# Cross attention of a two-block transformer kernel: heads made as channels, exponentials scaled before their transposes, and a weights unit moved between logits and transposes

## The chip, the cores and the metric

One core of a Trainium2 chip. The metric is the device time of one execution in microseconds (us), median of the runs. Everything is float32: matrix products of streamed weights are made in three passes of split numbers (high x high, high x low, low x high, marked fp32r), attention products in plain float32.

## What is computed

The kernel computes two transformer layers' worth of blocks on 256 tokens of width 1024. The part that the change touches is the memory cross attention of the first block:

```python
def memory_cross_attention(x, mem, norm_g, mem_g, wq, wk, wv, wo):
    h = rms_norm(x, norm_g)
    m = rms_norm(mem, mem_g)
    q = (h @ wq).reshape(B_, S, MEM_HEADS, MEM_HEAD_DIM)     # 4 heads of 256
    k = (m @ wk).reshape(B_, M, MEM_HEADS, MEM_HEAD_DIM)     # 256 memory rows
    v = (m @ wv).reshape(B_, M, MEM_HEADS, MEM_HEAD_DIM)
    logits = jnp.einsum('bshd,bmhd->bhsm', q, k) * (MEM_HEAD_DIM ** -0.5)
    p = jax.nn.softmax(logits, axis=-1)
    o = jnp.einsum('bhsm,bmhd->bshd', p, v)
    return o.reshape(B_, S, MEM_HEADS * MEM_HEAD_DIM) @ wo
```

The second block has memory attentions of its own, whose keys and values come from `a_mem_kv_2` and `b_mem_kv_2`; the kernel makes them early, beside this cross attention.

## The kernel before

**The stream of weights.** All weights pass through a ring of 4 places in units of 128 x 2048 numbers (1 MB). SP issues the transfer of unit u once unit u-4 is used. ACT copies it to the high part (`hi`, L2321, `w_hi`), DVE subtracts to get the low part (`lo`, L1497, `w_lo`), PE multiplies. On ACT and DVE the helper `product(name, i)` of unit u asks for the parts up to unit u+2 (AHEAD = 3). Each engine executes its own instructions strictly in the order in which the program lists them; the order of the work is therefore the order of the calls in `tensor_program`, `vector_program`, `scalar_program`, and semaphores (`Signal`) join them.

**The stage of the cross attention.** Queries (`cross_qT`) and keys (`cross_kT`) lie as channels (partitions) by tokens, values (`cross_v`) as rows. Around the attention the jobs `kv_m0` and `kv_m1` (two units each) make keys and values of the second block's memories in banks 0 and 1; `one_unit` (L898, L1734, L2470) hands out one unit per call, and before `kv_m1` begins PE waits until `kv_m0` has been copied out of the banks (`kept`): its keys by ACT (`memory_keys`, L2574), then its values by DVE (`memory_values`, L1846). The first unit of `kv_m0` runs on PE ahead of the attention; the other three are called from `attention("c", ...)` (L995, L1853, L2582).

In `attention` (L849, L1650, L2428) a head i goes through these steps, the steps of heads i, i-1 and i-2 lying in one pass i of the loop:
- PE makes the logits, 128 queries x 256 memory rows for each of two token tiles, in bank 4 or 5 (L859).
- DVE takes the maximum of each row (L1705), scaled by the inverse rms (L1711); ACT takes exponentials with their sums (L2441).
- PE transposes the exponentials in four blocks of 128 x 128 (L880, waits for the exponentials); ACT copies them to `weights_t` (L2459).
- PE multiplies, transposed exponentials stationary and values moving, giving tokens x 256 columns of the head (L893).
- DVE has made the inverse of the sums (L1661) and scales the head by it on the way out of the bank to `xn` (L1726, signal `o`).

The pass ends with `unit()`. In PE's pass 0 there is no unit, since the first has gone ahead; on ACT and DVE pass 0 has one, behind exponentials 0 and maxima 0.

**Behind the attention.** PE transposes the 16 blocks of `xn` (`turns("oc", ...)`, L998, executed at L697), ACT and DVE split them out of the banks to `oc_channels_hi` and `oc_channels_lo` (L2356, L1533), PE transposes the keys of the two memories (`heads_turned("mk0"/"mk1")`, 8 blocks, L843), and the output projection `co0`, `co1` (L1006, L1007) follows with the channels of `oc` moving.

Of the kernel before, what the change touches and what calls it, by code (L numbers as in the profile page):

```python
# [7 lines left out]
F32 = mybir.dt.float32  # L8
# [186 lines left out]
TURNS = {"mix": FULL, "mem": FULL, "mixed": FULL, "mem2": FULL, "oc": FULL, "lat": [(0, 0, 2), (1, 0, 2)],  # L195
# [5 lines left out]
class Kernel:  # L201
# [7 lines left out]
    def signals(self):  # L209
# [94 lines left out]
        self.o = Signal(nc, "heads_out", **iters)  # L304
        self.weighed = Signal(nc, "exps_normed", l=MLA_HEADS)
# [57 lines left out]
    def memory(self):  # L363
# [13 lines left out]
        def in_channels(name, kb, shape):  # L377
# [46 lines left out]
                   for n, kb in (("mixed", 64), ("oc", 8), ("bmix", 33))}  # L424
# [254 lines left out]
def tensor_program(k):  # L679
    nc, PE, bank, ident = k.nc, k.nc.tensor, k.bank, k.ident[:, :]  # L680

    def matmul(out, lhs, rhs, start, stop):
        return nc.tensor.matmul(out, lhs, rhs, start=start, stop=stop)  # L683
# [165 lines left out]
    def attention(tag, between=None, after=0):  # L849
        n, step, spans, off, total, dv = k.attention(tag)  # L850
        bias = ATTENTIONS[tag][2]
        for i in range(n + 2 + after):
            if i < n and tag in ("c", "l"):
                if i >= 2:
                    PE.wait_ge(*(k.maxed if bias else k.exped).at(tag, i - 2))
                for tok in range(NT):
                    for kk in range(2 if tag == "c" else 1):
                        lhs, rhs = k.logit_operands(tag, i, tok, kk)
                        m = matmul(bank[4 + i % 2][:, off[tok]:off[tok] + spans[tok]], lhs, rhs, kk == 0, tag != "c" or kk == 1)  # L859
                m.then_inc(k.qk.sem, 1)  # L860
            elif i < n and (step == 2 or i % 2 == 0):

                h0 = i * step
                for h in (h0, h0 + 1):
                    if h >= 2:
                        PE.wait_ge(*(k.maxed if bias else k.exped).at(tag, h - 2))
                for tok in range(NT):
                    for h in (h0, h0 + 1):
                        lhs, rhs = k.logit_operands(tag, h, tok, 0)
                        m = matmul(bank[4 + h % 2][:, off[tok]:off[tok] + spans[tok]], lhs, rhs, True, True)  # L870
                        if tok == NT - 1:
                            m.then_inc(k.qk.sem, 1)
# [122 lines left out]
    attention("c", lambda i: unit() if i else None)  # L995
    PE.wait_ge(*k.exped.all("c"))
    PE.wait_ge(*k.pt.all("c"))
    turns("oc", (0, 1, 2, 3), k.o.all("c"))  # L998
    kept("kv_m0")
    kept("kv_m1")  # L1000
    for n in range(2):
        PE.wait_ge(*k.ch_hi.at("oc", n))
        PE.wait_ge(*k.ch_lo.at("oc", n))
        heads_turned(f"mk{n}", [(k.mk_rows[n][:, tok, b * P:(b + 1) * P], P) for b in range(2) for tok in range(NT)], (4 + n,))
    PE.wait_ge(*k.o.all("c"))
    channel_job("co0", k.OC["oc"], "oc")  # L1006
# [486 lines left out]
def vector_program(k):  # L1493
# [156 lines left out]
    def attention(tag, between=None, finish=None):  # L1650
# [3 lines left out]
        def stat(j):  # L1654
            return k.stats[:, j % 4, :]
# [26 lines left out]
        def maxima(heads):  # L1682
            for h in heads:
# [25 lines left out]
                if tag == "c":  # L1709
                    V.wait_ge(*k.rstd_done.all("cross"))  # L1710
                    r = V.tensor_tensor(stat(h)[:, 0:2], stat(h)[:, 0:2], k.rstd_cols("cross"), ALU.mult)  # L1711
                else:
                    r = V.tensor_scalar(stat(h)[:, 0:2], stat(h)[:, 0:2], scale, None, ALU.mult)
                r.then_inc(k.maxed.sem, 1)
# [138 lines left out]
    attention("c", lambda i: unit())  # L1853
    channels_lo("oc", (0, 1, 2, 3))
# [462 lines left out]
def scalar_program(k):  # L2317
# [110 lines left out]
    def attention(tag, between=None, finish=None):  # L2428
        n, step, spans, off, total, dv = k.attention(tag)
        bias = ATTENTIONS[tag][2]  # L2430
        def exponentials(heads):
            for h in heads:
# [7 lines left out]
                for tok in range(NT):  # L2440
                    e = A.activation(E[:, off[tok]:off[tok] + spans[tok]], L[:, off[tok]:off[tok] + spans[tok]], ACT.Exp,  # L2441
                                     bias=stat[:, tok:tok + 1],
                                     scale=-1.0 if bias else k.rstd_cols("cross")[:, tok:tok + 1] if tag == "c" else k.scale_of(tag),
# [138 lines left out]
    attention("c", lambda i: unit())  # L2582
    channels_hi("oc", (0, 1, 2, 3))
    for n in range(2):
        heads_copied(f"mk{n}", 0, k.mem_kT[n][:, :, :])
    residual_job("co0", 0)
# [541 lines left out]
```

## Time and profile before

| | |
|---|---|
| median of 3 runs | 1156.02 us (1154.36 to 1156.06) |
| the profiled execution's own time | 1156.42 us |
| its span, first to last instruction | 1155.1 us |
| PE busy | 1117.1 us (97%), clock 0.992 of full |
| PE weight load busy | 1063.4 us (92%) |
| DVE, ACT, POOL busy | 732.8, 569.0, 73.4 us |
| 16 DMA engines | 182.70 MB, mean 158 GB/s |

The time of the profiled execution is its span and 1.3 us around it. PE is busy nearly throughout; the ends of its matmuls are modelled by the profiler, so pace is better read from start to start. A matmul of float32 operands shows as two instructions in the trace.

### The profile page before, as it was taken

What the parts mean: (1) busy time and instruction counts of PE and PEld (TensorE: products, weight loads), DVE (VectorE), ACT (ScalarE), POOL (GpSimd) and SP (SyncE); (2) the same over time, 40 slices, a digit from 0 to 9 for tenths busy, and PEclk for the clock granted to TensorE, in tenths of its full rate; (3) what the DMA queues carried; (4) which work ended last, traced back from release to release, by engine and by line L of the source; (5) the groups of instructions that cost most, each with busy time, mean ns of one, the idle gap of its engine ahead of it and who ended that gap; (6) DMA issues with size and microseconds to landing.
All of it is one profiled execution on the core that took longest, in us unless ns stands there. A gap on an engine that the chain in (4) does not pass through costs nothing.

```text
span 1155.1 us, 22499 instructions
## 1 busy us (share of the span) xinstructions
PE 1117.1 (97%) x9837; PEld 1063.4 (92%) x9837; DVE 732.8 (63%) x1042; ACT 569.0 (49%) x767; POOL 73.4 (6%) x134
## 2 busy tenths in 40 slices
PE   8999999999999999999799999999999999999998
PEld 8888889789999999988688999999987889999998
DVE  5557657455665556767988756555577875655553
ACT  6355646344544444684344634434365774443343
POOL 2410111100000000400000000000002000000000
PEclk9999999999999999998999999999999999999999
DMA  7933444325455554533000445555554224555551
GB/s 263 311 145 125 162 166 172 142 90 186 183 190 189 186 183 182 198 125 136 12 3 3 162 180 184 187 184 192 188 198 151 105 76 181 185 185 186 188 189 55
DMA packets 29862, 182.70 MB, mean 158 GB/s; under 512 B 3591, under 2 KB 6872, under 8 KB 8900
## 3 DMA queue, kind: packets, MB, share of 16 engines
q1 hardware_dynamic: 24608, 174.07, 41.8%
q0 software_dynamic: 1888, 4.75, 1.5%
q10 hardware_dynamic: 3268, 2.43, 0.7%
q8 instruction: 78, 1.28, 0.5%
q14 instruction: 20, 0.16, 0.0%
HBM read 180.18 MB, written 1.07 MB: 157 GB/s over the span
## 4 chain that ended last, share of the span: by engine, by line
PE 82%; DVE 7%; ACT 5%; issue 3%; POOL 2%; DMA 1%; ACTq 0%; DVEq 0%; POOLq 0%
PE bank L683 79%; ACT w_hi L2329 2%; DVE w_lo L1503 1%; DMA w_raw<-in_weights 1%; PE bank L697 1%; PE bank L880 1%; ACT exps L2441 1%; DVE inverse L2219 1%; DVE inverse_t L2244 0%; POOL inverse_rms_diagonals L2872 0%; DMA bias_rows<-bias_lines 0%; PE bank L687 0%; DVE chunk_products L2199 0%; PE bank L1225 0%; ACTq L2516 0%
## 5 line engine op out<-in xcount | busy, mean ns | idle before, releaser
L1503 DVE TENSOR_TENSOR w_lo<-w_raw,w_hi 128x2048 fp32r<-128x2048 f32 x157 | 358.0, 2291 | 200.1 <-ACT w_hi L2329 199.8
L2329 ACT ACTIVATE w_hi<-w_raw 128x2048 fp32r<-128x2048 f32 x161 | 306.5, 1913 | 111.4 <-DMA w_raw<-in_weights 106.2
L683 PE MATMUL bank<-x_channels_hi,w_hi 128*128 128x256 f32 x1424 | 230.8, 286 | 3.8 <-DVE proj L1575 1.3
L683 PE MATMUL bank<-x_channels_lo,w_hi 128*128 128x256 f32 x1424 | 228.3, 284 | 0.0
L683 PE MATMUL bank<-x_channels_hi,w_lo 128*128 128x256 f32 x1424 | 220.8, 278 | 0.0
L683 PEld LDWEIGHTS bank<-x_channels_hi,w_hi 128*128 128x128 f32 x1424 | 196.2, 192 | 7.6 <-issue 3.9
L683 PEld LDWEIGHTS bank<-x_channels_lo,w_hi 128*128 128x128 f32 x1424 | 194.2, 191 | 0.1
L683 PEld LDWEIGHTS bank<-x_channels_hi,w_lo 128*128 128x128 f32 x1424 | 191.7, 189 | 0.0
L683 PE MATMUL bank<-hidden_hi,w_lo 128*128 128x256 f32 x528 | 103.6, 284 | 0.0
L683 PE MATMUL bank<-hidden_hi,w_hi 128*128 128x256 f32 x528 | 102.0, 281 | 0.0
L683 PE MATMUL bank<-hidden_lo,w_hi 128*128 128x256 f32 x528 | 101.7, 280 | 0.0
L683 PEld LDWEIGHTS bank<-hidden_lo,w_hi 128*128 128x128 f32 x528 | 79.7, 188 | 0.0
L683 PEld LDWEIGHTS bank<-hidden_hi,w_hi 128*128 128x128 f32 x528 | 79.2, 188 | 0.5 <-issue 0.5
L683 PEld LDWEIGHTS bank<-hidden_hi,w_lo 128*128 128x128 f32 x528 | 79.5, 188 | 0.0
L2598 ACT ACTIVATE gates<-gates 128x512 f32<-128x512 f32 x33 | 20.9, 632 | 91.1 <-DVE gates L1877 91.1
L2602 ACT ACTIVATE hidden_hi<-values 128x512 fp32r<-128x512 f32 x33 | 20.9, 632 | 90.6 <-DVE values L1884 90.6
L1879 DVE TENSOR_TENSOR values<-bank,inverse_rms_rows 128x512 f32<-128x512 f32 x33 | 22.7, 689 | 40.7 <-PE bank L683 40.7
L1877 DVE TENSOR_TENSOR gates<-bank,inverse_rms_rows 128x512 f32<-128x512 f32 x33 | 22.6, 684 | 24.9 <-ACT inverse_rms_rows L2422 24.9
L1886 DVE TENSOR_TENSOR hidden_lo<-values,hidden_hi 128x512 fp32r<-128x512 f32 x33 | 22.9, 693 | 23.1 <-ACT hidden_hi L2602 23.1
L2885 POOL TENSOR_SCALAR channel_inverse_rms<-channel_mean_squares 128x2 f32<-128x2 f32 x5 | 1.2, 231 | 552.3 <-DVE channel_mean_squares L1644 552.3
L2403 ACT ACTIVATE x_channels_hi<-x,gain_columns 128x256 fp32r<-128x256 f32 x40 | 17.7, 500 | 33.3 <-DVE x L1606 33.3
L1606 DVE TENSOR_TENSOR x<-bank,x 128x512 f32<-128x512 f32 x28 | 19.0, 687 | 21.9 <-PE bank L683 21.8
(450 smaller groups left out, 1550.1 us busy)
## 6 DMA issues: line engine op xcount, KB each, us to landing
w_raw<-in_weights SPq DMA_DIRECT2D x163, 1024.0 KB, 4.8
mem_rows<-in_mem POOLq DMA_DIRECT2D x2, 1024.0 KB, 6.1
xn<-in_x SPq DMA_DIRECT2D x1, 1024.0 KB, 5.5
w_raw<-in_weights SPq DMA_DIRECT2D x2, 512.0 KB, 8.6
bias<-bias_rows ACTq DMA_DIRECT2D x2, 512.0 KB, 9.1
bias<-bias_rows ACTq DMA_DIRECT2D x1, 1024.0 KB, 11.0
out<-xn SPq DMA_DIRECT2D x4, 256.0 KB, 2.5
wide_masks<-in_triangle_masks POOLq DMA_DIRECT2D x1, 832.0 KB, 8.3
```

What stands on the lines that cost most here:

```text
L683: return nc.tensor.matmul(out, lhs, rhs, start=start, stop=stop)
L697: t = nc.tensor.transpose(b[:, j * P:(j + 1) * P], k.turn_source(stage, tok, k0 + j), ident)
L880: m = nc.tensor.transpose(b[:, c:c + P], e[:, c:c + P], ident)
L1503: V.tensor_tensor(k.w_lo[:, s, :], k.w_raw[:, s, :], k.w_hi[:, s, :].bitcast(F32), ALU.subtract).then_inc(k.lo_done, 1)
L1606: V.tensor_tensor(k.x[:, b:b + 2, :], k.product_bank(name, n).rearrange("p (k t) -> p k t", k=2), k.x[:, b:b + 2, :], ALU.add).then_inc(k. ...
L1877: V.tensor_tensor(k.gates[:, par, :, :], pairs(2 * par), R, ALU.mult).then_inc(k.gate_scaled.sem, 1)
L1879: V.tensor_tensor(k.values[:, par, :, :], pairs(2 * par + 1), R, ALU.mult).then_inc(k.up_scaled.sem, 1)
L1886: V.tensor_tensor(k.HL[:, par, :, :], k.values[:, par, :, :], k.HH[:, par, :, :].bitcast(F32), ALU.subtract).then_inc(k.hid_lo.sem, 1)
L2329: A.activation(k.w_hi[:, s, :], k.w_raw[:, s, :], ACT.Copy).then_inc(k.hi_done, 1)
L2403: A.activation(high[:, b, :], k.x[:, b, :], ACT.Copy, scale=k.split_gain(stage, part, b)).then_inc(k.x_hi.sem, 1)
L2598: A.activation(k.gates[:, par, :, :], k.gates[:, par, :, :], ACT.Silu).then_inc(k.silu.sem, 1)
L2602: A.activation(k.HH[:, par, :, :], k.values[:, par, :, :], ACT.Copy).then_inc(k.hid_hi.sem, 1)
```

## The change

Cross attention no longer uses the general `attention`; each engine gets its own order, head by head. The head's output is made as channels x tokens at once: values stationary (two blocks of 128 channels), transposed exponentials moving (256 tokens, picked from `weights_t` in two runs of 128), so the 16 transposes of `xn` and the scaled copy to `xn` go. The exponentials are scaled by their inverse sums in SBUF before they are transposed. ACT and DVE split each head from its bank (`cross_heads_hi`, `cross_heads_lo`). On PE the second unit of `kv_m0` stands between the logits of head 1 and the transposes of head 0. On ACT and DVE the first `unit()` stands ahead of exponentials and maxima 0, and both of heads 0 and 1 ahead of the second. The `oc` channels move to other places of SBUF.

```diff
@@ -192 +192 @@
-TURNS = {"mix": FULL, "mem": FULL, "mixed": FULL, "mem2": FULL, "oc": FULL, "lat": [(0, 0, 2), (1, 0, 2)],
+TURNS = {"mix": FULL, "mem": FULL, "mixed": FULL, "mem2": FULL, "lat": [(0, 0, 2), (1, 0, 2)],
          "qlat": [(0, 0, 4), (1, 0, 4)], "bmix": [(0, 6, 2), (1, 6, 2)]}
 SPLITS = {"cross": 1, "ffn0": 1, "n1": 1, "ffn1": 1, "kvb": 2, "ffn2": 1}
@@ -301,8 +301,10 @@
...
-        self.o = Signal(nc, "heads_out", **iters)
-        self.weighed = Signal(nc, "exps_normed", l=MLA_HEADS)
+        self.o = Signal(nc, "heads_out", **{**iters, "c": 0})
+        self.weighed = Signal(nc, "exps_normed", c=4, l=MLA_HEADS)
+        self.cross_hi = Signal(nc, "cross_heads_hi", c=4)
+        self.cross_lo = Signal(nc, "cross_heads_lo", c=4)
...
@@ -421,7 +423,8 @@
...
+        self.OC["oc"] = (work("oc_channels_hi", 40, [P, KT, S], F32R), work("oc_channels_lo", 72, [P, KT, S], F32R))
...
@@ -850,15 +853,7 @@
         n, step, spans, off, total, dv = k.attention(tag)
...
-            if i < n and tag in ("c", "l"):
-                if i >= 2:
-                    PE.wait_ge(*(k.maxed if bias else k.exped).at(tag, i - 2))
-                for tok in range(NT):
-                    for kk in range(2 if tag == "c" else 1):
-                        lhs, rhs = k.logit_operands(tag, i, tok, kk)
-                        m = matmul(bank[4 + i % 2][:, off[tok]:off[tok] + spans[tok]], lhs, rhs, kk == 0, tag != "c" or kk == 1)
-                m.then_inc(k.qk.sem, 1)
-            elif i < n and (step == 2 or i % 2 == 0):
+            if i < n and (step == 2 or i % 2 == 0):
...
@@ -992,18 +987,57 @@
...
-    attention("c", lambda i: unit() if i else None)
-    PE.wait_ge(*k.exped.all("c"))
-    PE.wait_ge(*k.pt.all("c"))
-    turns("oc", (0, 1, 2, 3), k.o.all("c"))
+    def cross_logits(h):
+        if h >= 2:
+            PE.wait_ge(*k.exped.at("c", h - 2))
+        for tok in range(NT):
+            for kk in range(2):
+                lhs, rhs = k.logit_operands("c", h, tok, kk)
+                m = matmul(bank[4 + h % 2][:, tok * S:(tok + 1) * S], lhs, rhs, kk == 0, kk == 1)
+        m.then_inc(k.qk.sem, 1)
+    def cross_exps_turned(h):
+        PE.wait_ge(*k.weighed.at("c", h))
+        if h >= 2:
+            PE.wait_ge(*k.pt.at("c", h - 2))
+        e = k.exps("c", h)
+        for c in range(0, NT * S, P):
+            m = nc.tensor.transpose(bank[6 + h % 2][:, c:c + P], e[:, c:c + P], ident)
+        m.then_inc(k.e_turned.sem, 1)
+    def cross_values(h):
+        PE.wait_ge(*k.pt.at("c", h))
+        if h >= 2:
+            PE.wait_ge(*k.cross_lo.at("c", h - 2))
+        pt = k.ptbuf[:, (h % 2) * 512:(h % 2) * 512 + NT * S].rearrange("p (t j c) -> p t j c", t=NT, j=2)
+        for b in range(2):
+            for j in range(2):
+                m = matmul(bank[2 + h % 2][:, b * S:(b + 1) * S].rearrange("p (t c) -> p t c", t=NT),
+                           k.cross_v[:, j, 256 * h + P * b:256 * h + P * (b + 1)], pt[:, :, j, :], j == 0, j == 1)
+        m.then_inc(k.pv.sem, 1)
+    cross_logits(0)
+    for i in range(1, 4):
+        cross_logits(i)
+        unit()
+        cross_exps_turned(i - 1)
+        if i >= 2:
+            cross_values(i - 2)
+    cross_exps_turned(3)
+    cross_values(2)
     kept("kv_m0")
     kept("kv_m1")
+    PE.wait_ge(*k.exped.all("c"))
     for n in range(2):
-        PE.wait_ge(*k.ch_hi.at("oc", n))
-        PE.wait_ge(*k.ch_lo.at("oc", n))
         heads_turned(f"mk{n}", [(k.mk_rows[n][:, tok, b * P:(b + 1) * P], P) for b in range(2) for tok in range(NT)], (4 + n,))
-    PE.wait_ge(*k.o.all("c"))
-    channel_job("co0", k.OC["oc"], "oc")
+    cross_values(3)
+    PE.wait_ge(*k.cross_lo.at("c", 1))
+    channel_product("co0", 0, k.OC["oc"])
+    PE.wait_ge(*k.cross_lo.at("c", 3))
+    channel_product("co0", 1, k.OC["oc"])
     channel_job("co1", k.OC["oc"])
...
@@ -1850,8 +1879,52 @@
...
-    attention("c", lambda i: unit())
-    channels_lo("oc", (0, 1, 2, 3))
+    def cross_maxima(h):
+        stat = k.stats[:, h, :]
+        V.wait_ge(*k.qk.at("c", h))
+        for tok in range(NT):
+            k.dve.mark(V.tensor_reduce(out=stat[:, tok:tok + 1], in_=bank[4 + h % 2][:, tok * S:(tok + 1) * S], axis=AX.X, op=ALU.max,
+                                       negate=True))
+        V.wait_ge(*k.dve.so_far())
+        V.wait_ge(*k.rstd_done.all("cross"))
+        V.tensor_tensor(stat[:, 0:2], stat[:, 0:2], k.rstd_cols("cross"), ALU.mult).then_inc(k.maxed.sem, 1)
+    def cross_exps_normed(h):
+        stat, E = k.stats[:, h, :], k.exps("c", h)
+        V.wait_ge(*k.exped.at("c", h))
+        V.reciprocal(stat[:, 4:6], stat[:, 2:4]).then_inc(k.inverse.sem, 1)
+        V.wait_ge(*k.inverse.at("c", h))
+        for tok in range(NT):
+            cols = slice(tok * S, (tok + 1) * S)
+            r = V.tensor_scalar(E[:, cols], E[:, cols], stat[:, 4 + tok:5 + tok], None, ALU.mult)
+            if tok == 0:
+                k.dve.mark(r)
+        r.then_inc(k.weighed.sem, 1)
+    def cross_heads_lo(h):
+        high, low = k.OC["oc"]
+        V.wait_ge(*k.cross_hi.at("c", h))
+        V.tensor_tensor(low[:, 2 * h:2 * h + 2, :], bank[2 + h % 2][:, :].rearrange("p (k t) -> p k t", k=2),
+                        high[:, 2 * h:2 * h + 2, :].bitcast(F32), ALU.subtract).then_inc(k.cross_lo.sem, 1)
+    unit()
+    cross_maxima(0)
+    cross_maxima(1)
+    cross_exps_normed(0)
+    cross_exps_normed(1)
+    unit()
+    cross_maxima(2)
+    cross_exps_normed(2)
+    unit()
+    cross_maxima(3)
+    cross_heads_lo(0)
+    cross_exps_normed(3)
+    unit()
+    for h in range(1, 4):
+        cross_heads_lo(h)
...
@@ -2579,10 +2652,52 @@
...
-    attention("c", lambda i: unit())
-    channels_hi("oc", (0, 1, 2, 3))
+    def cross_exps(h):
+        E, stat = k.exps("c", h), k.stats[:, h, :]
+        A.wait_ge(*k.maxed.at("c", h))
+        if h >= 2:
+            A.wait_ge(*k.e_turned.at("c", h - 2))
+        for tok in range(NT):
+            cols = slice(tok * S, (tok + 1) * S)
+            e = A.activation(E[:, cols], bank[4 + h % 2][:, cols], ACT.Exp, bias=stat[:, tok:tok + 1],
+                             scale=k.rstd_cols("cross")[:, tok:tok + 1], accum_out=stat[:, 2 + tok:3 + tok])
+            if tok == 0:
+                k.act.mark(e)
+        e.then_inc(k.exped.sem, 1)
+    def cross_exps_kept(h):
+        A.wait_ge(*k.e_turned.at("c", h))
+        if h >= 2:
+            A.wait_ge(*k.pv.at("c", h - 2))
+        at = (h % 2) * 512
+        A.activation(k.ptbuf[:, at:at + NT * S], bank[6 + h % 2][:, :], ACT.Copy).then_inc(k.pt.sem, 1)
+    def cross_heads_hi(h):
+        A.wait_ge(*k.pv.at("c", h))
+        A.activation(k.OC["oc"][0][:, 2 * h:2 * h + 2, :], bank[2 + h % 2][:, :].rearrange("p (k t) -> p k t", k=2),
+                     ACT.Copy).then_inc(k.cross_hi.sem, 1)
+    unit()
+    cross_exps(0)
+    cross_exps(1)
+    unit()
+    cross_exps_kept(0)
+    cross_exps(2)
+    unit()
+    cross_exps_kept(1)
+    cross_exps(3)
+    cross_heads_hi(0)
+    unit()
+    cross_exps_kept(2)
+    cross_heads_hi(1)
+    cross_exps_kept(3)
+    cross_heads_hi(2)
     for n in range(2):
         heads_copied(f"mk{n}", 0, k.mem_kT[n][:, :, :])
+    cross_heads_hi(3)
     residual_job("co0", 0)
     residual_job("co1", 4)
```

## Rows read from the trace of the kernel before

**Rows 1.** The page: chain that ended last by engine; DMA issues, us to landing.

```profile
PE 82%; DVE 7%; ACT 5%; issue 3%; POOL 2%; DMA 1%; ACTq 0%; DVEq 0%; POOLq 0%
...
w_raw<-in_weights SPq DMA_DIRECT2D x163, 1024.0 KB, 4.8
```

**Rows 2.** Busy time of each engine in the stage: us, PE, PEld, DVE, ACT, POOL, PEclk, DMA.

```profile
212.20:251.20 39.00, 35.89 (x178) 29.50 (x176) 19.12 (x32) 18.13 (x33) 0.00 (x0) 1.00 0.30 108
```

**Rows 3.** Timeline of PE: start us, us, engine line op operands, [idle before <-releaser].

```profile
212.20 3.62 PE L683 MATMUL bank<-cross_kT,cross_qT 128*128 128x256 f32 x16
216.37 0.66 PE L880 MATMUL bank<-ident,exps 128*128 128x128 f32 x4 [0.55 <-ACT exps L2441]
216.78 1.18 PE L683 MATMUL bank<-w_hi,mem_channels_hi 128*128 128x512 f32 x4
...
222.44 1.89 PE L683 MATMUL bank<-cross_kT,cross_qT 128*128 128x256 f32 x8
224.16 0.60 PE L880 MATMUL bank<-ident,exps 128*128 128x128 f32 x4
224.60 1.89 PE L683 MATMUL bank<-cross_v,weights_t 128*128 128x256 f32 x8
227.98 1.20 PE L683 MATMUL bank<-w_hi,mem_channels_hi 128*128 128x512 f32 x4 [1.49 <-DVE mem_v L1850]
...
243.56 3.62 PE L683 MATMUL bank<-cross_v,weights_t 128*128 128x256 f32 x16
248.05 1.94 PE L697 MATMUL bank<-ident,xn 128*128 128x128 f32 x16 [0.88 <-DVE xn L1726]
250.18 1.23 PE L843 MATMUL bank<-ident,mem_k_rows 128*128 128x128 f32 x8 [0.19 <-DVE oc_channels_lo L1533]
251.16 0.72 PE L683 MATMUL bank<-oc_channels_hi,w_hi 128*128 128x256 f32 x4
```

**Rows 4.** Timeline of ACT in the same stage.

```profile
215.11 0.56 ACT L2441 ACTIVATE exps<-bank,stats,channel_inverse_rms 128x256 f32<-128x256 f32 x1 [10.52 <-DVE stats L1711]
...
216.21 1.91 ACT L2329 ACTIVATE w_hi<-w_raw 128x2048 fp32r<-128x2048 f32 x1
...
221.33 0.56 ACT L2441 ACTIVATE exps<-bank,stats,channel_inverse_rms 128x256 f32<-128x256 f32 x1 [3.22 <-DVE stats L1711]
...
224.71 0.84 ACT L2579 ACTIVATE mem_k_rows<-bank,row_inverse_rms 128x256 f32<-128x256 f32 x2
```

**Rows 5.** Timeline of DVE in the same stage.

```profile
214.12 0.75 DVE L1705 TENSOR_REDUCE stats<-bank 128x1 f32<-128x256 f32 x2 [6.62 <-PE bank L683]
...
218.14 2.29 DVE L1503 TENSOR_TENSOR w_lo<-w_raw,w_hi 128x2048 fp32r<-128x2048 f32 x1 [3.07 <-ACT w_hi L2329]
220.35 0.74 DVE L1705 TENSOR_REDUCE stats<-bank 128x1 f32<-128x256 f32 x2
...
224.85 2.29 DVE L1503 TENSOR_TENSOR w_lo<-w_raw,w_hi 128x2048 fp32r<-128x2048 f32 x1 [3.48 <-ACT w_hi L2329]
227.06 0.87 DVE L1850 TENSOR_SCALAR mem_v<-bank,row_inverse_rms 128x256 f32<-128x256 f32 x2
```

**Rows 6.** Groups of DVE between 800 and 1000 us: xcount | busy us, mean ns.

```profile
L2025 DVE TENSOR_SCALAR exps<-exps,stats 128x256 f32<-128x256 f32 x12 | 4.2, 347 | 0.0
```

**Rows 7.** Groups between 205 and 256 us: `oc` split by DVE and ACT, reciprocals.

```profile
L1533 DVE TENSOR_TENSOR oc_channels_lo<-bank,oc_channels_hi 128x512 fp32r<-128x512 f32 x4 | 2.5, 682 | 1.4 <-ACT oc_channels_hi L2356 1.4
...
L2356 ACT ACTIVATE oc_channels_hi<-bank 128x512 fp32r<-128x512 f32 x4 | 2.1, 602 | 4.4 <-PE bank L697 4.4
...
L1661 DVE RECIPROCAL stats<-stats 128x2 f32<-128x2 f32 x4 | 0.6, 157 | 0.0
```

**Rows 8.** Timeline of PE at an earlier block of transposes.

```profile
154.37 1.06 PE L697 MATMUL bank<-ident,xn 128*128 128x128 f32 x8 [0.89 <-ACT cross_v L2381]
156.66 1.68 PE L697 MATMUL bank<-ident,xn 128*128 128x128 f32 x8 [1.23 <-DVE xn L1826]
```

**Rows 9.** Busy time of each engine around those transposes, columns as in rows 2.

```profile
155.00:160.00 5.00, 3.77 (x21) 3.54 (x20) 3.29 (x6) 3.30 (x5) 1.82 (x4) 0.70 0.92 327
```

More of the change, by code:

```diff
@@ L423, in memory @@
         self.OC = {n: (work(f"{n}_channels_hi", kb, [P, KT, S], F32R), work(f"{n}_channels_lo", kb + 8, [P, KT, S], F32R))
-                   for n, kb in (("mixed", 64), ("oc", 8), ("bmix", 33))}
+                   for n, kb in (("mixed", 64), ("bmix", 33))}
+        self.OC["oc"] = (work("oc_channels_hi", 40, [P, KT, S], F32R), work("oc_channels_lo", 72, [P, KT, S], F32R))
         self.OC["amix"] = (work("amix_channels_hi", 36, [P, KT, S], F32R), work("amix_channels_lo", 60, [P, KT, S], F32R))
@@ L1708, in maxima @@
                 V.wait_ge(*k.dve.so_far())
[L1709 to L1714, printed above, removed]
+                V.tensor_scalar(stat(h)[:, 0:2], stat(h)[:, 0:2], scale, None, ALU.mult).then_inc(k.maxed.sem, 1)
         for i in range(n + 2 + (finish is not None)):
@@ L2442, in exponentials @@
                                      bias=stat[:, tok:tok + 1],
-                                     scale=-1.0 if bias else k.rstd_cols("cross")[:, tok:tok + 1] if tag == "c" else k.scale_of(tag),
+                                     scale=-1.0 if bias else k.scale_of(tag),
                                      accum_out=stat[:, 2 + tok:3 + tok])
```

## The prediction

> **What bounds the kernel now.** I read the page first: PE makes 82% of the chain that ended last [rows 1], so a saving counts only where it shortens PE's own row of work. The busy shares by stage come next: in the cross attention's 39.0 us, from its first logits to the first product of `co0`, PE shows 35.9 us busy at full clock (1.00), DVE 19.1 and ACT 18.1 [rows 2]. The waits are thus few, but there are some, and PE's timeline puts four of them in their places [rows 3]: 0.55 us for the exponentials of head 0, 1.49 us for `mem_v`, 0.88 us for the last scaled head in `xn`, 0.19 us for the `oc` split. The timelines of ACT and DVE say where the largest is from. Maxima 0 end before 215.1, exponentials 0 run to 216.2, and only behind them does ACT make a `w_hi` (216.21) [rows 4] and DVE its `w_lo` (218.14); maxima 1, though their logits have been ready since 216, stand behind that until 220.35, and so exponentials 1 until 221.33, the next `w_hi`, the next `w_lo` until 224.85, and `mem_v` until 227.06 [rows 4, 5]. PE must not start `kv_m1` ahead of `mem_v`, and starts at 227.98.
>
> **PE's work after the change, by pace.** Starts give these prices [rows 3]: a head's logits 1.72 us (222.44 to 224.16, 8 instructions at 0.215), four transposes 0.44 us (224.16 to 224.60), a unit of `kv_m` about 5.6 us (216.78 to 222.44, less a few hundredths at its start). A head's values are 8 instructions of the same shape and the same shown length as the logits (1.89 us for 8 in both rows), so 1.72. The eight transposes of memory keys cost 0.87 at 0.108 each; their 0.98 (250.18 to 251.16) has a small wait in it.
> What stays is 4 x 1.72 of logits, 4 x 1.72 of values, 4 x 0.44 of transposes, 3 units x 5.6, and 0.87: 33.2 us. With no wait anywhere `co0` starts at 212.20 + 33.2 = 245.4. It starts at 251.16 now. The difference is **5.75 us**. From the other side: the 16 transposes of `xn` are 1.7 us, the four waits 3.1 us, and about 0.9 us are the drains that come with a wait (the next instruction starts some 0.2 us after the pace of those before it would let it) and the slower first instructions behind one. So both ways agree.
>
> **Is there really no wait?** This is the step on which all hangs, so I carried the three queues forward together, with a hand-over from PE of 0.2 us (logits 0 are paced out at 213.92, the maxima start at 214.12 [rows 3, 5]) and of 0.03 between ACT and DVE.
> - *The first unit moved ahead.* Its `w_hi` and `w_lo` are for two units on. The transfer is issued when the unit four before is used, that is two units of 5.6 us ahead of 212.2, near 201, and lands 4.8 us later [rows 1], at 206. ACT sat idle for 10.52 us before 215.11 and DVE for 6.62 before 214.12 [rows 4, 5], so the 1.9 and 2.3 us fit there for nothing. Were they late, logits 0 would wait with them; there are 4 us to spare.
> - *Heads 0 and 1.* Maxima 0 at 214.12, exponentials 0 to 216.2; maxima 1 at 215.84 in place of 220.35, exponentials 1 at 216.83 to 217.9. The scalings of exponentials are new: two instructions of 0.35 us each [rows 6] behind a reciprocal of 0.16 us [rows 7], 0.9 us a head. Head 0 is scaled by 217.7, head 1 by 218.9. PE, meanwhile at logits 1 and then the second unit of `kv_m0` until 221.24, wants head 0 at 221.24: 3.5 us of cover. The 0.55 us wait is gone with the unit that now lies there.
> - *The narrow place.* ACT's next `w_hi` runs 217.9 to 219.85, then the keys of `kv_m0`, the second at 221.41 (unit's end and hand-over) to 221.9; DVE's `w_lo` 219.9 to 222.15, then two `mem_v`, 0.87 us [rows 5], to 223.0. PE has turned head 0 (221.68) and made logits 2 (223.40) by then: 0.4 us to spare, where 1.49 us were waited.
> - *Head 3*, whose scaling on DVE is behind the low part of head 0: logits 3 end at 232.9, maxima to 234.05, exponentials to 235.15, ACT's high part of head 0 0.60 us, DVE's low part 0.68 us [rows 7], scaling to 237.4. PE wants it at 240.6.
> - *The end.* `kept` of the second unit of `kv_m1` at 240.9, wanted at 242.8; `weights_t` of head 2 at 239.7, wanted at 241.1; of head 3 at 242.05, wanted at 243.7. `co0`'s first half needs heads 0 and 1 (split at 242.2), its second half head 3, split at 246.9 and wanted 5.6 us after the first, at 251.0. That split moved to the cover of `co0`; ACT's and DVE's parts for `co1`, which stand behind it, come as long after the start of `co0` as now, some 7 us, and are wanted at 11.
> ACT trades four copies (`oc`) for four of the same size, DVE four scaled copies to `xn` and four splits for eight scalings and four splits: the scalings cost 3.5 us a stage, the `xn` copies were 2.7, on an engine that has 20 us free in this stage [rows 2]. No transfer is added or moved; SP's queue follows PE.
> **Behind the stage** nothing is tied to absolute time: every transfer is issued on PE's progress. I take the whole 5.75 us to the end, since PE makes the chain there too.
>
> **A rule weighed against the rows.** From 247.0 (the pace of the last values) to 251.16 PE of before does only transposes and waits, and the granted clock is 1.00 throughout [rows 2, 3]. Around 154 to 158 it did the same, 16 transposes with idle time between, and there the clock went to its lower level (1.2 of 2.4 GHz; 0.70 as mean of 5 us, so 5 x 0.30 = 1.5 us lost) [rows 8, 9]. The change takes the 4 us stretch away.
> The Trainium skill's page "TensorE: Matmul & The Clock Gate", section "Part 4: PE-mode transpose", says that transposes don't count as PE being busy for the clock. By that rule executions of before can lose clock at 247 to 251 too, and the saving would be about 7.3 us; the trace of this stage disagrees (1.00), that of 154 to 158 agrees.
>
> **New and unseen in the trace: the moving operand in two runs of 128.** The values product now streams `weights_t` in two pieces of 512 B, 1 KB apart, and writes a bank through a two-part pattern. No row shows a float32 product so fed. Bounds: nothing (the same 8 instructions of 256 columns), or twice the pace, 6.9 us in all for 32 instructions [rows 3]; less than nothing is excluded, for the columns streamed are the same. I take nothing: the nearest row is the values product itself.
>
> **The sum.** 1156.42 (the profiled execution) - 5.75 = 1150.67. That execution stood 0.4 us above the median of the runs, so the median goes from 1156.02 to **1150.3**.
>
> **Rivals.**
> 1. *A wait comes back in part.* The narrow place is 0.4 us wide. If exponentials 1 or the `w_hi` behind them come 2 us later than I have it, PE waits 1.6 us for `mem_v` again, as it waited 1.49; a like slip can happen at `weights_t` of head 2 (1.4 us to spare). 1156.02 - 4.1 = 1151.9. For: in-order queues with many hand-overs. Against: each duration is measured in this very stage.
> 2. *More than forecast.* Where before's ordinary runs lose clock in the transposes at 247 to 251, 1.5 us more are saved: 1148.8. For: the lowest run is 1.7 us under the median, about one such loss. Against: the profiled execution has no loss there and is not faster than the others.
> 3. *Slower.* The values products, in their new form, run at half pace, as between the two bounds above. They lie on PE's own row with nothing to cover them: +6.9 - 5.75 = +1.15 us, 1157.2. It decides from about 0.18 us more per instruction (5.75 / 32) on a pace of 0.215. Against: nothing in the rows; the pace of products here is set by the columns.
> 4. *The change does not do what it says:* the transposes of the exponentials now wait for DVE, not for ACT, and the saved waits return as waits for DVE. For: four such waits are new. Against: cover of 3 us at each. It would leave only the `xn` transposes and their waits, some 3.2 us (from 247.0 to 250.18): 1152.8.
>
> **How the numbers follow.** Forecast 0.70, rival 1 0.11, rival 2 0.09, rival 3 0.03, rival 4 0.07. A measurement of this kernel can tell about 0.2% from no change, 2.3 us. All but rival 3 are faster by more than that, if rivals 1 and 4 do not go together with other slips; I give the same 0.06, slower 0.02. The range takes in rival 1 and rival 2 and about half of rival 4: 1148.6 to 1152.5.
>
> **What would show it.** In the changed profile: no `PE L697` group on `xn` in this stage; `co0`'s first product 33 us behind the first logits; PE's waits between them under 0.5 us; values products at 0.215 us each from start to start; scalings at 0.35 us and maxima 1 directly behind maxima 0; `mem_v` of `kv_m0` done within 0.4 us of the end of logits 2. A values row of 8 instructions that takes 3.4 us to the next start would prove rival 3, a wait for `mem_v` or `weights_t` rival 1, a wait for the scaled `exps` rival 4. A span behind `co0` that differs from before's by over 1 us would say that the saving is not carried to the end.

## The result, and the profile after

| | before | after |
|---|---|---|
| median of 4 runs each, side by side | 1155.71 us (1154.36 to 1156.06) | 1148.26 us (1147.11 to 1149.09) |
| ratio, 95% interval | | 0.9937 (0.9920 to 0.9954) |
| the profiled execution's own time | 1156.42 us | 1147.55 us |
| its span | 1155.1 us | 1146.2 us |
| first logits to first product of `co0` | 38.96 us | 32.99 us |

Faster by 0.63%, or 7.5 us between these medians. The prediction was 1150.3 us, with a range from 1148.6: the direction and nearly all of the mechanism came out as forecast, and the time lies 0.3 us below the range.

The page after, chain by engine and the transfers of weights, answers to [rows 1]: PE still sets the end, and no transfer was touched.

```profile
PE 83%; DVE 7%; ACT 4%; issue 2%; POOL 2%; DMA 1%; ACTq 0%; DVEq 0%; POOLq 0%
...
w_raw<-in_weights SPq DMA_DIRECT2D x163, 1024.0 KB, 4.8
```

Busy time in the stage after, from the first logits to `co0`, with the columns of [rows 2]:

```profile
211.06:244.05 32.99, 32.99 (x162) 27.91 (x160) 17.14 (x34) 16.78 (x32) 0.00 (x0) 1.00 0.35 128
```

PE shows as busy in all 32.99 us. Its timeline after shows the new order, and no row in it carries an idle time in brackets, where [rows 3] had four:

```profile
211.06 3.62 PE L686 MATMUL bank<-cross_kT,cross_qT 128*128 128x256 f32 x16
214.32 1.28 PE L686 MATMUL bank<-w_hi,mem_channels_hi 128*128 128x512 f32 x4
...
220.09 0.60 PE L1007 MATMUL bank<-ident,exps 128*128 128x128 f32 x4
220.53 1.89 PE L686 MATMUL bank<-cross_kT,cross_qT 128*128 128x256 f32 x8
222.07 1.27 PE L686 MATMUL bank<-w_hi,mem_channels_hi 128*128 128x512 f32 x4
...
227.82 0.60 PE L1007 MATMUL bank<-ident,exps 128*128 128x128 f32 x4
228.26 1.89 PE L686 MATMUL bank<-weights_t,cross_v 128*128 128x256 f32 x8
229.99 1.89 PE L686 MATMUL bank<-cross_kT,cross_qT 128*128 128x256 f32 x8
231.53 1.29 PE L686 MATMUL bank<-w_hi,mem_channels_hi 128*128 128x512 f32 x4
...
237.30 0.60 PE L1007 MATMUL bank<-ident,exps 128*128 128x128 f32 x4
237.74 1.89 PE L686 MATMUL bank<-weights_t,cross_v 128*128 128x256 f32 x8
239.47 0.60 PE L1007 MATMUL bank<-ident,exps 128*128 128x128 f32 x4
239.90 1.89 PE L686 MATMUL bank<-weights_t,cross_v 128*128 128x256 f32 x8
241.63 1.04 PE L846 MATMUL bank<-ident,mem_k_rows 128*128 128x128 f32 x8
242.50 1.89 PE L686 MATMUL bank<-weights_t,cross_v 128*128 128x256 f32 x8
244.05 0.81 PE L686 MATMUL bank<-oc_channels_hi,w_hi 128*128 128x256 f32 x4
```

ACT's timeline after (against [rows 4]): the first `w_hi` has gone into the idle time ahead of the attention, and exponentials 1 stand directly behind exponentials 0.

```profile
204.41 1.92 ACT L2402 ACTIVATE w_hi<-w_raw 128x2048 fp32r<-128x2048 f32 x1 [0.96 <-DMA w_raw<-in_weights]
213.97 0.56 ACT L2663 ACTIVATE exps<-bank,stats,channel_inverse_rms 128x256 f32<-128x256 f32 x1 [7.64 <-DVE stats L1891]
...
215.70 0.56 ACT L2663 ACTIVATE exps<-bank,stats,channel_inverse_rms 128x256 f32<-128x256 f32 x1 [0.52 <-DVE stats L1891]
...
216.79 1.92 ACT L2402 ACTIVATE w_hi<-w_raw 128x2048 fp32r<-128x2048 f32 x1
```

DVE's timeline after (against [rows 5]): maxima 1 at 214.71 behind maxima 0 at 212.98, the scalings, then `w_lo` and `mem_v`, which end at 221.83. PE starts `kv_m1` at 222.07. That 0.24 us is the narrow place that the prediction named.

```profile
206.36 2.29 DVE L1537 TENSOR_TENSOR w_lo<-w_raw,w_hi 128x2048 fp32r<-128x2048 f32 x1
212.98 0.76 DVE L1887 TENSOR_REDUCE stats<-bank 128x1 f32<-128x256 f32 x2 [4.33 <-PE bank L686]
...
214.71 0.76 DVE L1887 TENSOR_REDUCE stats<-bank 128x1 f32<-128x256 f32 x2 [0.78 <-PE bank L686]
...
215.77 0.62 DVE L1901 TENSOR_SCALAR exps<-exps,stats 128x256 f32<-128x256 f32 x2
...
218.75 2.29 DVE L1537 TENSOR_TENSOR w_lo<-w_raw,w_hi 128x2048 fp32r<-128x2048 f32 x1 [1.00 <-ACT w_hi L2402]
220.96 0.87 DVE L1879 TENSOR_SCALAR mem_v<-bank,row_inverse_rms 128x256 f32<-128x256 f32 x2
```

**The rest of the time.** The span fell by 8.9 us, the stage by 5.97. The other 2.9 us lie ahead of the stage (1.1 us) and behind it (1.8 us), where PE's order is unchanged. Much of this follows the granted clock. Three stretches of before, with the columns of [rows 2]:

```profile
150.00:165.00 15.00, 12.88 (x81) 11.65 (x81) 10.64 (x11) 7.77 (x12) 2.66 (x6) 0.89 0.49 180
520.00:535.00 15.00, 15.00 (x85) 13.24 (x84) 11.59 (x17) 9.37 (x11) 0.00 (x0) 0.77 0.32 108
...
870.00:880.00 10.00, 8.14 (x39) 6.81 (x38) 8.03 (x10) 3.98 (x7) 4.06 (x5) 0.83 0.30 107
```

and the same of after:

```profile
150.00:165.00 15.00, 12.88 (x93) 11.56 (x92) 10.98 (x12) 8.10 (x12) 2.99 (x7) 1.00 0.54 192
515.00:530.00 15.00, 15.00 (x100) 13.61 (x100) 13.50 (x23) 9.56 (x16) 0.00 (x0) 0.89 0.32 123
...
870.00:880.00 10.00, 9.20 (x48) 6.91 (x47) 7.11 (x25) 8.06 (x16) 0.96 (x2) 1.00 0.53 193
```

Length times (1 - clock) gives the loss of a stretch: about 1.7, 3.4 and 1.7 us in before's profiled execution, 0, 1.7 and 0 in after's. Is that a gift of the change, or of the one execution that was profiled? The copies below answer most of this.

### The profile page after: what moved, and what is told of

The parts are those of the page before. It is cut to its first block, busy times and chain, and to the rows that moved or that the text cites. A ratio compares the mean times of both kernels' runs of the same rounds, so it can differ in the third digit from the quotient of the medians.

```text
span 1146.2 us, 22461 instructions
## 1 busy us (share of the span) xinstructions
PE 1112.4 (97%) x9821; PEld 1060.4 (93%) x9821; DVE 733.3 (64%) x1046; ACT 569.4 (50%) x767; POOL 73.4 (6%) x134
## 3 DMA queue, kind: packets, MB, share of 16 engines
HBM read 180.18 MB, written 1.07 MB: 158 GB/s over the span
## 4 chain that ended last, share of the span: by engine, by line
PE 83%; DVE 7%; ACT 4%; issue 2%; POOL 2%; DMA 1%; ACTq 0%; DVEq 0%; POOLq 0%
PE bank L686 80%; DVE w_lo L1537 1%; ACT w_hi L2402 1%; DMA w_raw<-in_weights 1%; PE bank L700 1%; PE bank L875 1%; DVE inverse L2292 1%; DVE inverse_t L2317 0%; ACT exps L2514 0%; POOL inverse_rms_diagonals L2987 0%; DMA bias_rows<-bias_lines 0%; PE bank L690 0%; DVE chunk_products L2272 0%; PE bank L1259 0%; PE bank L1278 0%
```

## The experiments

Every kernel ran beside runs of the kernel before on the same chip. "Stage" is always the first logits to the first product of `co0`, by PE's timeline.

### Both kernels again, unchanged: e1_before_again, e8_before_third, e11_before_fourth, e2_after_again, e9_after_third, e10_after_fourth

No edit. These show what one kernel's profile and median do from copy to copy.

> The kernel before once more, unchanged, for its spread and for where its clock falls. In the two first profiles the stage from the first logits to co0 took 38.96 us before and 32.99 after, 5.97 less, but the spans differ by 8.9 and the medians by 7.45. Theory A (chance): the 1.5 to 3 us that are left are granted clock lost at places that differ from execution to execution (before: near 155, 525, 571, 873 us; after: near 525, 568, 1133). Then this profile has another set of such places than the first, and time plus half-clock loss (span x (1 - mean clock)) is near 1147.2 in every execution of this kernel. Theory B (rival 2 of the prediction): ordinary executions of this kernel lose clock at 247 to 255 us, in the transposes that the change takes away. Then this profile shows a clock under 1.00 in that stretch. Theory C: the change costs or gives time outside its stage by itself; then the places are the same as in the first profile, stage by stage.

> The changed kernel once more, unchanged. Stage from first logits to co0 again 33.0 us by every theory. A: the places of lost clock differ from those of its first profile, and the ratio over ten or so runs of each moves towards the stage's 5.97 us (0.9948), time less clock loss near 1141.1. B: ratio stays near 0.9937 (7.3 us less), and the places other than 247 to 255 are as frequent in both kernels. C: same places as in its first profile, none near 155 and 873 us, ratio stays near 0.9937.

> The kernel before a third time, for the number of its executions that lose clock. Theory A: spans differ from those of the changed kernel, at equal loss, by the stage's 5.97 us; this profile again shows no lower clock at 247 to 255 us, and its places of loss differ from the two others. Rival 2: it does show it.

> The changed kernel again, for the 1 us between the stage (5.97 us less in every profile) and the medians (7.45, 6.6 less). Theory A (chance): clock is lost in pieces at the same few loss-prone places in both kernels, which of them are hit differs from execution to execution; over more runs the difference comes down towards 6.0 us, about 0.9948, and segment by segment the profile equals the others but for a piece lost here and there. Theory C (something of the change outside the stage): it stays at 7.

> As the run before it; a second sample on the same chip. By theory A the two samples of the same kernel differ from each other by as much as either from 6.0 us less than before, some tenths to 1 us; by theory C both are 7 us less, alike.

> The kernel before again beside them. By theory A a copy of before differs from before by tenths as well, and its stage is 38.96 to 39.00 us with the clock at 1.00 in it.

| kernel | median (range, runs) | ratio to before, side by side | stage | clock low at (us from start) |
|---|---|---|---|---|
| before | 1155.71 (1154.36-1156.06, 4) | 1 | 38.96 | 157, 526-532, 570, 874, 1154 |
| e1, before | 1155.47 (1152.30-1159.59, 12) | 1.0008 (0.9995-1.0021) | 38.99 | 555, 565-572, 1145 on |
| e8, before | 1154.19 (1152.06-1156.17, 11) | 1.0006 (0.9997-1.0015) | 39.00 | 527, 568, 1145 on |
| e11, before | 1154.30 (1151.98-1157.01, 12) | 0.9997 (0.9987-1.0007) | 38.97 | 553, 567, 1144, 1151 |
| after | 1148.26 (1147.11-1149.09, 4) | 0.9937 (0.9920-0.9954) | 32.99 | 520, 561, 1138 on |
| e2, after | 1147.91 (1146.69-1148.35, 5) | 0.9938 (0.9926-0.9951) | 33.00 | 157, 550, 560-567, 1140 on |
| e9, after | 1147.89 (1146.19-1149.72, 6) | 0.9940 (0.9927-0.9954) | 32.99 | 101, 159, 552, 562-569, 1142 on |
| e10, after | 1146.92 (1146.28-1147.66, 5) | 0.9932 (0.9920-0.9944) | 32.98 | 157, 549, 563, 1140 |

Each place named is a piece of 3.4 us (6.8 where two numbers stand; "on": to the end, less in the last place of before and of e11, which the end cuts off), in which the clock is at its lower level (1.2 of 2.4 GHz). Two stretches of e1, which is the kernel before, and of e2, which is the changed one:

```profile
150.00:165.00 15.00, 12.89 (x93) 11.57 (x92) 10.91 (x12) 8.19 (x12) 3.02 (x8) 1.00 0.55 198
...
870.00:880.00 10.00, 8.62 (x46) 6.93 (x47) 7.41 (x11) 4.92 (x8) 1.97 (x3) 1.00 0.40 144
```

```profile
150.00:165.00 15.00, 12.88 (x82) 11.70 (x81) 10.90 (x11) 7.67 (x12) 2.57 (x6) 0.89 0.46 174
```

At 150 to 165 us the copy of before is at full clock and the copy of after is not: the other way round than in the two profiles above. So the losses there belong to the execution, not to the kernel. The stage, in contrast, is 38.96 to 39.00 in four profiles and 32.98 to 33.00 in four. **The change takes 5.97 us out of the stage.** Of the 2.9 us outside it in the first pair of profiles, much is chance: from `co0`'s first product to the end, the four profiles of before take 901.4 to 904.6 us, those of the changed kernel 901.0 to 902.2. It is not shown that all of it is. The expectations had said that by chance alone the ratio would come towards 0.9948; the places of low clock moved as that theory said, but the ratios stayed at 0.9938, 0.9940 and 0.9932, and the last interval does not hold 0.9948. What is left of this stands under "What stays open".

The clock in the transposes at the end of before's stage is 1.00 in all four profiles. Here e8, from the values of head 2 to well behind `co0`'s start:

```profile
240.00:260.00 20.00, 18.93 (x137) 17.32 (x136) 11.38 (x13) 8.30 (x12) 0.00 (x0) 1.00 0.27 100
```

### e3_rows_back: the form of the heads as before, the new order kept

```diff
-        PE.wait_ge(*k.weighed.at("c", h))
+        PE.wait_ge(*k.exped.at("c", h))
...
-                m = matmul(bank[2 + h % 2][:, b * S:(b + 1) * S].rearrange("p (t c) -> p t c", t=NT),
-                           k.cross_v[:, j, 256 * h + P * b:256 * h + P * (b + 1)], pt[:, :, j, :], j == 0, j == 1)
+                m = matmul(bank[2 + h % 2][:, tok * S:(tok + 1) * S], pt[:, tok * S + j * P:tok * S + (j + 1) * P],
+                           k.cross_v[:, j, 256 * h:256 * h + 256], j == 0, j == 1)
...
     cross_exps_turned(3)
     cross_values(2)
+    cross_values(3)
...
+    turns("oc", (0, 1, 2, 3), k.o.all("c"))
...
-    cross_values(3)
```

with the scaled copies to `xn` and the splits of `oc` as before, and no scaling of exponentials.

> The new order of the three queues kept, but heads made as rows again: exponentials not scaled, transposed exponentials stationary and values moving, head scaled into xn by DVE, 16 transposes of xn, split from there, co0 behind. Theory (PE's row of work sets the time): back come 16 transposes (1.73 us), the wait for the last head in xn (about 0.9), that for the split (0.2), and some 0.3 of drains: stage 33.0 + 3.2 = 36.2 us, 1151.4 us. The waits of 0.55 and 1.49 us stay away. If instead the order alone had given nothing and all came from the form, it would be at the time before, 1155.7. By rival 2 of the prediction another 1.5 us are lost in some executions in the transposes at their new place, 242 to 247 us.

Measured: 1151.13 us (1150.45 to 1152.75, 6 runs), ratio 0.9971 (0.9959 to 0.9984); stage 36.45 us. Its PE timeline has the tail of [rows 3] back, with the same two waits:

```profile
245.29 1.94 PE L700 MATMUL bank<-ident,xn 128*128 128x128 f32 x16 [0.88 <-DVE xn L1904]
247.42 1.23 PE L846 MATMUL bank<-ident,mem_k_rows 128*128 128x128 f32 x8 [0.19 <-DVE oc_channels_lo L1568]
248.40 0.72 PE L686 MATMUL bank<-oc_channels_hi,w_hi 128*128 128x256 f32 x4
```

The form of the heads is worth 36.45 - 32.99 = 3.46 us of the stage: 16 transposes (1.73 us at 0.108 each), 1.07 us of waits, and some 0.7 us that come with the waits. The expectation had 3.2 us.

### e4_order_back: the old order on all three engines, the new heads kept

```diff
         cross_logits(i)
-        unit()
         cross_exps_turned(i - 1)
         if i >= 2:
             cross_values(i - 2)
+        unit()
```

and on ACT and DVE `unit()` behind exponentials 0 and maxima 0, then one behind each further head, as before.

> The other half: heads as channels, exponentials scaled, but the order of before on all three queues: exponentials of a head turned directly behind the next head's logits and ahead of the unit, the first weights unit of ACT and DVE behind exponentials and maxima 0. Theory: PE waits for the scaling of head 0 (0.55 + 0.8 us of scaling = about 1.4) and for mem_v before kv_m1 (1.5 or somewhat more, since scalings now stand in DVE's queue): stage 33.0 + 3 = 36.0 us, 1151.2 us. If the form alone carried the gain it would stay at 1148.3.

Measured: 1149.15 us (1148.66 to 1153.63, 6 runs), ratio 0.9959 (0.9943 to 0.9974); stage 35.54 us. PE's two waits:

```profile
215.75 0.66 PE L1007 MATMUL bank<-ident,exps 128*128 128x128 f32 x4 [1.40 <-DVE exps L1901]
...
226.52 1.19 PE L686 MATMUL bank<-w_hi,mem_channels_hi 128*128 128x512 f32 x4 [0.65 <-DVE mem_v L1879]
```

The order is worth 35.54 - 32.99 = 2.55 us. The two halves add up: 3.46 + 2.55 = 6.01, against 5.97 for both. The first wait is 1.40 here and was 0.55 in [rows 3]: in the old order the scaling in front of the transposes is not covered and costs 0.85 us. In the new order it has a unit of `kv_m0` over it. Yet the new heads gain as much without the new order, 38.96 - 35.54 = 3.42 us, as on top of it: what the wait for the scaling costs, the wait for `mem_v` gives back (0.65 us here, 1.49 in [rows 3]).

### e7_scaled_twice: each exponential scaled a second time, by 1.0

```diff
-            r = V.tensor_scalar(E[:, cols], E[:, cols], stat[:, 4 + tok:5 + tok], None, ALU.mult)
+            k.dve.mark(V.tensor_scalar(E[:, cols], E[:, cols], stat[:, 4 + tok:5 + tok], None, ALU.mult))
+        V.wait_ge(*k.dve.so_far())
+        for tok in range(NT):
+            cols = slice(tok * S, (tok + 1) * S)
+            r = V.tensor_scalar(E[:, cols], E[:, cols], 1.0, None, ALU.mult)
```

> Each scaling of exponentials on DVE is done, and then once more by 1.0: two further instructions of about 0.3 us and a wait for each head, some 0.7 us of delay. Theory (scaling is covered by the weights unit on PE, 2.5 us and more to spare at each head): stage 33.0 to 33.1 us, no change in time. Rival 4 of the prediction (PE waits for DVE's scaling): up to 4 x 0.7 = 2.8 us more. The narrow place, mem_v 0.2 us ahead of PE, isn't touched, since DVE idled 1.0 us for w_hi behind head 1's scaling.

Measured: 1147.02 us (1146.57 to 1147.33, 4 runs), ratio 0.9937 (0.9921 to 0.9952); stage 32.99 us, to 0.01 us that of the changed kernel. DVE's timeline shows the second scalings running in what was idle time:

```profile
217.13 0.62 DVE L1901 TENSOR_SCALAR exps<-exps,stats 128x256 f32<-128x256 f32 x2
217.78 0.50 DVE L1905 TENSOR_SCALAR exps<-exps 128x256 f32<-128x256 f32 x2
218.75 2.29 DVE L1537 TENSOR_TENSOR w_lo<-w_raw,w_hi 128x2048 fp32r<-128x2048 f32 x1 [0.47 <-ACT w_hi L2406]
```

`w_lo` starts at 218.75 with or without them, because it waits for ACT's `w_hi`, not for DVE. The scalings are covered, with at least the 0.50 us of a second pair to spare.

### e12_unit_behind: only the first unit's place on ACT and DVE put back

```diff
-    unit()
     cross_maxima(0)
+    unit()
     cross_maxima(1)
```

and the same around `cross_exps(0)` on ACT. PE's order is the new one.

> The changed kernel with one thing undone: on ACT and DVE the first weights unit stands again behind exponentials 0 and maxima 0 (PE's order and the form of the heads are kept). Theory (it is the order of the queues that removes the 1.49 us wait): maxima 1 come 4.5 us later, behind w_lo; head 0 is scaled 0.9 us after PE wants it, and the keys and values of kv_m0 are out about 3.2 us after PE wants bank 0. Stage 33.0 + 4 = 37.0 us, 1152. If PE's new order alone carries the gain, nothing changes.

Measured: 1153.71 us (1151.27 to 1156.31, 11 runs), ratio 0.9991 (0.9981 to 1.0002): nothing measurable is left of the gain. Stage 38.77 us. PE's timeline:

```profile
221.00 0.66 PE L1007 MATMUL bank<-ident,exps 128*128 128x128 f32 x4 [0.69 <-DVE exps L1901]
221.49 1.89 PE L686 MATMUL bank<-cross_kT,cross_qT 128*128 128x256 f32 x8
226.42 1.93 PE L686 MATMUL bank<-w_hi,mem_channels_hi 128*128 128x512 f32 x4 [3.04 <-DVE mem_v L1879]
228.15 1.91 PE L686 MATMUL bank<-w_lo,mem_channels_hi 128*128 128x512 f32 x4
229.86 1.18 PE L686 MATMUL bank<-w_hi,mem_channels_lo 128*128 128x512 f32 x4
```

and the stretch behind the long wait:

```profile
226.00:231.00 5.00, 4.58 (x13) 3.61 (x14) 2.67 (x8) 3.01 (x5) 0.00 (x0) 0.66 0.00 0
```

Two things happen. `mem_v` is late by the whole length of a unit's copies, as maxima 1 again stand behind `w_hi` and `w_lo`: 3.04 and 0.69 us of waits. Then, behind the long wait, the granted clock falls to its lower level for 3.4 us from 226.6 on: four products start 1.73 us apart where four take 0.93 elsewhere, and the loss is 5 x 0.34 = 1.7 us. Without it the stage would be 37.07, an estimate, and the expectation, which left the clock out, had 37.0. Put against e4: putting back one unit on ACT and DVE alone costs 5.8 us (4.1 without the clock), putting back the order on all engines 2.55. The three queues' orders are one change.

### e5_turns_added and e6_products_added: 8 us of transposes, or of products, ahead of `co0`

```diff
     cross_values(3)
     PE.wait_ge(*k.cross_lo.at("c", 1))
+    warm(74, 6)
+    for _ in range(19):
+        matmul(bank[6][:, 0:S], ident, k.cross_v[:, 0, 0:S], True, True)
     channel_product("co0", 0, k.OC["oc"])
```

The first added line, 74 transposes of `ident`, is e5's; the loop, 19 float32 products (38 instructions), is e6's. Their results are used by nobody. If transposes let the clock fall, e5 shows it in this stretch and e6 does not.

> The changed kernel with 74 transposes of the identity put on PE between the last values and co0 (74 x 0.108 = 8.0 us), a stretch like the one of before (16 transposes and waits, 247 to 251 us) but longer. Stage 33.0 + 8.0 = 41.0 us by every theory, if the clock stays. By rival 2 of the prediction (transposes let the clock fall) the windows at 245 to 255 us show the lower clock, and the run is slower than the one with as long a stretch of products by 1 to 4 us: about 1158 to 1160. By chance alone (theory A) both added kernels take 1156.0 and lose clock in this stretch equally seldom.

> The same place filled with 19 float32 products of 128 x 256 (38 instructions of 0.215 us, 8.2 us) in place of transposes; their result is not used. Both theories: stage 41.2 us, clock 1.00 there, 1156.2 us. It is the ruler for the run with transposes.

Measured: e5 1158.36 us (1156.49 to 1159.56, 5 runs), ratio 1.0034 (1.0021 to 1.0047), stage 41.17; e6 1157.09 us (1156.16 to 1159.10, 11 runs), ratio 1.0026 (1.0017 to 1.0034), stage 41.19. Busy time and clock in e5's added transposes, and in e6's added products:

```profile
247.44:251.44 4.00, 4.00 (x38) 4.00 (x37) 2.04 (x2) 3.80 (x3) 0.00 (x0) 1.00 0.00 0
251.44:255.43 3.99, 3.99 (x39) 3.99 (x38) 3.15 (x2) 0.42 (x1) 0.00 (x0) 1.00 0.00 0
```

```profile
243.89:251.90 8.01, 8.01 (x39) 7.05 (x38) 5.19 (x3) 4.20 (x3) 0.00 (x0) 1.00 0.00 0
```

Eight microseconds of nothing but transposes leave the clock at its full level, as eight of products do. Against the changed stage e5 adds 8.18 us and e6 8.20, and the medians rise by rather more: 10.5 and 9.2 us against 1147.9, the changed kernel's median in e2 and e9.

e5's median is thus 1.3 us above e6's, and it lies where the expectation had put it by rival 2 (1158 to 1160). Its profile shows another place. The stage starts 3.2 us later than in the changed kernel's first profile (214.26, not 211.06), with code that is the same up to there, since the clock is low at 101 and at 159 us:

```profile
100.00:105.00 5.00, 4.09 (x22) 3.47 (x23) 3.33 (x13) 3.12 (x11) 0.00 (x0) 0.66 0.00 0
...
156.29:161.29 5.00, 3.62 (x22) 3.42 (x23) 2.83 (x6) 3.01 (x9) 2.25 (x5) 0.78 0.82 292
```

By the mean granted clock of each execution, 9.7 us are lost to the clock in e5's and 8.8 in e6's, against 7.5 in the changed kernel's, which is the size of the surplus. Where the executions without a profile lost it is not shown.

## Why the prediction was right, and where it was wrong

**PE's row without waits: right, 0.2 us too long.** "33.2 us" was measured as 32.99. By terms, from start to start: logits 6.34 us (6.88 predicted), three units 17.29 (16.8), transposes 1.75 (1.76), values 6.74 (6.88), keys 0.87 (0.87). The two errors are one: where a unit follows 8 logits it starts after 1.54 us, not 1.72, and the unit then takes 0.15 us longer to its own end. Before's profile had such a pair once, in a row that [rows 3] leaves out: values at 235.83, a unit at 237.37, and 5.75 us until the next block. What is left over, 0.2 us, is mostly the last values: `co0` starts 1.55 us after them, not 1.72.

**"Is there really no wait?": right at every station.** With the stage's start moved from 212.20 to 211.06, the carried times less 1.14 are: `w_hi` 216.76 (measured 216.79), `w_lo` 218.76 (218.75), end of `mem_v` 221.86 (221.83). The later ones came as well or up to 0.3 us sooner: head 3 scaled at 236.04 (236.26), `mem_v` of the second unit of `kv_m1` at 239.51 (239.76), `weights_t` of head 2 at 238.54 (238.56), the last split at 245.76 (245.76). Only PE came sooner than thought at the narrow place (222.07, not 222.26), so it is 0.24 us wide and not 0.4. A scaled head costs DVE 0.62 us and its reciprocal 0.16, where 0.9 in all was taken.

**Rival 1, a wait comes back: not in this kernel.** e12 shows how near it lies: one call in another place on two engines, and the wait is 3.04 us.

**Rival 2, clock lost at 247 to 251 in ordinary runs of before: not seen at that place.** The measured time is almost this rival's (1148.8), but not by its mechanism, as far as profiles show: clock 1.00 there in four profiles of before, in e3, and in 8 us of transposes in e5. The executions without a profile have only a mean clock, and e5's median, 1.3 us above e6's, does not speak against the rival. The rule weighed in the prediction (the Trainium skill, "TensorE: Matmul & The Clock Gate", "Part 4: PE-mode transpose": transposes don't count as the engine being busy) does not agree with these rows of float32 transposes. The fall around 157 came with waits between the transposes [rows 8] (with waits of 0.89 and 1.22 us the clock stayed full there in e1), and the one in e12 behind a wait of 3 us in a stretch without any `xn` transposes; that idle time is what matters there is consistent with both but wasn't tested alone.

**Rival 3, values at half pace: refuted.** Eight instructions of values start 1.73 us ahead of what follows (228.26 to 229.99), as in the old form.

**Rival 4, waits for the scalings: refuted in the new order** by e7, and true to 0.85 us in the old one, by e4.

**The step that failed** is the last: "That execution stood 0.4 us above the median of the runs, so the median goes from 1156.02 to 1150.3". It took the level from three runs and gave it no error. Over all 101 executions of the kernel before in this study the median is 1154.3 us, 1.7 us below the 1156.02 of the three. (In the four runs beside the changed kernel it is 1155.71, 0.3 us below, and the difference there is 7.45 us.) From 1154.3, the predicted 5.75 us lead to 1148.5 and the measured 5.97 to 1148.3. That this is the measured 1148.26 is partly luck: over its 20 executions the changed kernel's median is 1147.7. Against that, the forecast was 2.6 us too high: 1.7 for the level, 0.2 for the stage, and some 0.7 outside the stage, which the sum put at nothing and which no run explains.

The range was made from the rivals and the operation costs alone. But single executions of one unchanged kernel spread over 1152 to 1159.6, in good part because pieces of low clock outside the stage come and go: where such a piece is in one profile and not in the other, the stretch differs by about as much (the memory normalisation's, 52.7 us long, takes 54.3 with the piece at 157). The standard deviation of one execution is 1.5 us, and a median of three carries about 1 us of it (an estimate from these 101).

"I take the whole 5.75 us to the end" holds where the clock is full: from `co0`'s first product to the product with `inverse_rms_diagonals` seven of the eight profiles take 234.0 to 234.2 us, of either kernel. The eighth, e8, takes 235.2 at clock 1.00, with a wait of 0.62 us for `hidden_hi` at 456 that no other has: not every difference between copies is the clock.

**What stays open.** Over 20 executions the changed kernel's mean is 1147.7 us (standard error 0.2), over 101 the kernel before's is 1154.5 (0.15): 6.8 us, where the stage gives 5.97. The mean granted clock of the executions does not explain it: 0.6 to 0.7% of the span is lost by it with both kernels. Copies of one kernel themselves differ by up to 1.5 us in their medians (1155.71 and 1154.19), so it can be chance. In the eight profiles it lies behind `co0`, where before takes 903.4 us on average and the changed kernel 901.4, and ahead of the stage it is the other way (211.3 and 212.3). One place stands out: from ACT's last `w_hi` to the end before takes 27.0 us in its first profile, and 29.8 in e8, where the clock is low in the last 9.5 us. Four profiles of each are too few to tell chance from an effect of the change.

## What to carry to other kernels

When several in-order engines feed each other, carry all their queues forward together on one clock, from measured durations and hand-overs: here that gave each of three stations within 0.03 us, and it named the narrow place. A reorder has to be made in every queue that takes part: moving the unit on PE and leaving the first one behind on ACT and DVE was worse than no move (e12 against e4), and a new operation on the side (the scalings) is free only under a cover. And before a saving of half a per cent is turned into a time, learn how far single executions of the unchanged kernel spread: the level of three runs was off by more than a quarter of the saving.

## What the runs showed of the hardware that was not expected

- Transposes kept the clock: 74 float32 transposes of 128 x 128 and nothing else, 8.0 us, ran at clock 1.00 (e5's profile), at 0.108 us each.
- A single wait of 3.04 us, in a stage that otherwise ran at full clock, was followed by 3.4 us at the lower level: 1.7 us lost on top of the wait (e12). The waits of 1.49 to 1.51 us in this stage of before had no such effect in any of four profiles.
- The same program falls to the lower clock in different places from one execution to the next (101, 157, 520 to 532, 550 to 572, 874, the end), by 3.4 or 6.8 us at a time, and for up to 9.5 us at the end (e8). A piece at 101, 157 or 874 cost 1.5 to 1.6 us against the profiles without it; between 550 and 572 a second piece cost 0.4 us or less.
- A float32 product whose moving operand comes in two runs of 128 columns, and whose result goes to the bank in two, ran at the pace of the plain one (0.216 us an instruction).
